# Moving three pieces of work around the gated recurrence of a hybrid backbone kernel: the third weight split, the order of the scans, and the gate rows

## The reference, cut to what matters

```python
xr, yr, qkv, z, beta_raw, alpha_raw = jnp.split(h @ w_in, EVEN_SPLITS, axis=-1)
xr = dw_conv(xr, lru_cw, lru_cb)
q, k, v = jnp.split(jax.nn.silu(dw_conv(qkv, dn_cw)), ...)

def lru_gates(xc, w_a, b_a, w_i, b_i, lam):       # for each of two directions d
    r = sigmoid(blockwise(xc, w_a) + b_a)
    i = sigmoid(blockwise(xc, w_i) + b_i)
    log_a = -LRU_C * r * softplus(-lam)
    a = exp(log_a)
    b = sqrt(-expm1(2.0 * log_a)) * (i * xc)
    return a, b                                   # then h[t] = a[t] * h[t-1] + b[t]
...
lru = (h_forward + h_backward) * gelu(yr)
```

## Time and profile before

| what | us |
|---|---|
| median of 3 runs | 1379.16 |
| lowest and highest of them | 1378.51, 1383.32 |
| the profiled execution's own time | 1377.73 |
| its span, first to last instruction | 1375.9 |
| PE busy | 1342.9 |
| DVE, ACT, POOL busy | 860.0, 693.1, 289.0 |
| recurrence's bodies b = 0 to 7 in the span | 84.7 to about 286 |

### The profile page before, as it was taken

How to read it: one execution, slowest core, us unless ns; L and a number is a source line. 1 busy time by engine, 2 the same in 40 slices (tenths; PEclk the granted TensorE clock), 3 DMA queues, 4 the chain that set the end, 5 groups by cost and what they waited for, 6 DMA issues and landing times.

```text
span 1375.9 us, 27903 instructions
## 1 busy us (share of the span) xinstructions
PE 1342.9 (98%) x11206; PEld 1265.3 (92%) x11206; DVE 860.0 (63%) x1320; ACT 693.1 (50%) x1100; POOL 289.0 (21%) x296
## 2 busy tenths in 40 slices
PE   6999999999999999999999999999999999999998
PEld 4889999998899999999899999999998988899997
DVE  4745889985456555543587666566736665664664
ACT  5367888868544455422533312343126665653543
POOL 2000124412566787621100000000120001100002
PEclk9999999999999999999999999999999999999999
DMA  9632232231411110123466566565423211455652
GB/s 326 200 86 85 78 92 77 78 93 62 143 43 32 59 35 31 63 77 100 138 194 192 183 197 190 184 197 180 138 92 122 93 62 47 154 183 185 187 188 99
DMA packets 138030, 170.88 MB, mean 124 GB/s; under 512 B 10912, under 2 KB 121760, under 8 KB 137920
## 3 DMA queue, kind: packets, MB, share of 16 engines
q1 hardware_dynamic: 137312, 169.13, 38.9%
q0 software_dynamic: 608, 0.19, 0.1%
HBM read 168.25 MB, written 1.05 MB: 123 GB/s over the span
## 4 chain that ended last, share of the span: by engine, by line
PE 81%; ACT 8%; DVE 5%; POOL 2%; issue 2%; DMA 1%; SPq 0%; ACTq 0%; POOLq 0%; DVEq 0%
PE bank L2324 59%; PE bank L2678 3%; PE bank L2666 3%; ACT w_hi L887 1%; PE bank L2250 1%; POOL qkv L741 1%; PE bank L2695 1%; DVE w_lo L1523 1%; DVE qkv L1565 1%; PE bank L2910 1%; ACT l_i L1153 1%; PE bank L2620 1%; PE bank L2933 1%; PE bank L2542 1%; PE bank L2644 1%
## 5 line engine op out<-in xcount | busy, mean ns | idle before, releaser
L1523 DVE TENSOR_TENSOR w_lo<-raw,w_hi 128x1024 fp32r<-128x1024 f32 x216 | 269.6, 1248 | 324.3 <-ACT w_hi L887 323.8
L887 ACT ACTIVATE w_hi<-raw 128x1024 fp32r<-128x1024 f32 x216 | 228.4, 1058 | 427.1 <-PE bank L2324 426.9
L2324 PE MATMUL bank<-h_hi,w_hi 128*128 128x256 f32 x1728 | 374.2, 283 | 13.6 <-DVE w_lo L1523 5.5
L2324 PE MATMUL bank<-h_hi,w_lo 128*128 128x256 f32 x1728 | 367.0, 279 | 0.0
L2324 PE MATMUL bank<-h_lo,w_hi 128*128 128x256 f32 x1728 | 359.9, 279 | 0.0
L2324 PEld LDWEIGHTS bank<-h_hi,w_hi 128*128 128x128 f32 x1728 | 277.2, 190 | 24.4 <-issue 16.7
L2324 PEld LDWEIGHTS bank<-h_hi,w_lo 128*128 128x128 f32 x1728 | 275.2, 189 | 0.0
L2324 PEld LDWEIGHTS bank<-h_lo,w_hi 128*128 128x128 f32 x1728 | 271.7, 189 | 0.3 <-DVE h_lo L1746 0.2
L709 POOL TENSOR_TENSOR n_sq<-xT 128x512 f32<-128x512 f32 (+1 forms) x24 | 23.3, 972 | 719.5 <-DVE xT L1593 718.6
L2324 PE MATMUL bank<-hid_hi,w_hi 128*128 128x256 f32 x768 | 172.9, 279 | 0.1
L2324 PE MATMUL bank<-hid_hi,w_lo 128*128 128x256 f32 x768 | 171.7, 278 | 0.0
(11 more groups left out here) (318 smaller groups left out, 2138.6 us busy)
## 6 DMA issues: line engine op xcount, KB each, us to landing
raw<-in_mlp_w SPq DMA_DIRECT2D x128, 512.0 KB, 3.6
late_w<-in_w_mod SPq DMA_DIRECT2D x56, 512.0 KB, 4.4
raw<-in_even_w_in SPq DMA_DIRECT2D x48, 512.0 KB, 3.7
raw<-in_w_mod SPq DMA_DIRECT2D x24, 512.0 KB, 4.4
first_w<-in_w_mod SPq DMA_DIRECT2D x16, 512.0 KB, 11.3
raw<-in_even_w_out SPq DMA_DIRECT2D x16, 512.0 KB, 3.4
raw<-in_attn_w_qkv SPq DMA_DIRECT2D x16, 512.0 KB, 3.6
raw<-in_attn_w_o SPq DMA_DIRECT2D x8, 512.0 KB, 3.5
```

What stands on the lines that cost most here:

```text
L887: act.activation(w_hi[:, j % SPLIT], raw[:, j % RAW], ACT.Copy).then_inc(hi_ready, 1)
L1523: dve.tensor_tensor(w_lo[:, j % SPLIT], raw[:, j % RAW], w_hi[:, j % SPLIT].bitcast(F32), ALU.subtract).then_inc(split_done, 1)
L2324: return pe.matmul(bank[2 * pair + t][:, c - n0:c - n0 + CTX], w[:, slot, k, t * P:(t + 1) * P], x_[:, c:c + CTX], start=(kk == 0 and firs ...
```

## The change

There are four edits.

1. PE: the gate rows and their signal `s_gps` move from behind `xr` to a place ahead of the fourth first unit (n = 3). The copy on ACT to `gate_f` moves with them, from behind `xr` to between its two bodies.
2. ACT: in bodies 0 to 7 the eight sigmoids are cut into two fours by direction, and the split of u2 goes between them.
3. ACT: the two tanhs go behind the split of u3, instead of ahead of it.
4. DVE: in all bodies but b = 8 the split of u2 goes ahead of `lru_output` of the tile before (its scans, sum and product), instead of behind it.

```diff
--- before.py
+++ after.py
@@ -1060,8 +1060,12 @@
                 ends = b == LRU_TILES + 1
                 beside(b, 0)
                 split_hi(u + 2, 2)
+                if b < LRU_TILES:
+                    lru_gates(b, 1)
                 beside(b, 1)
                 split_hi(u + 3, 3)
+                if b < LRU_TILES:
+                    lru_tanh(b)
                 evac(s, it, 0)
                 if b >= LRU_TILES:
                     value_silus(BY_POOL + 4 * (b - LRU_TILES))
@@ -1138,26 +1142,26 @@
 
                 act.wait_ge(s_lam, 1)
                 act.activation(sp_b[:, 64:80], sp_a[:, 64:80], ACT.Exp, scale=-1.0).then_inc(s_lam, 1)
+                act.wait_ge(s_gps, 1)
+                act.activation(gate_f[:, :], bank[X2][:, :], ACT.Copy).then_inc(s_gate, 1)
 
             segment(SEG["xr"], done=2, behind=decays_and_gates)
-            act.wait_ge(s_gps, 1)
-            act.activation(gate_f[:, :], bank[X2][:, :], ACT.Copy).then_inc(s_gate, 1)
-
-            def lru_gates(t_):
-
-                act.wait_ge(s_lps, t_ + 1)
-                act.wait_ge(l_w, t_)
-                act.wait_ge(l_x, t_)
+
+            def lru_gates(t_, d):
+
+                if d == 0:
+                    act.wait_ge(s_lps, t_ + 1)
+                    act.wait_ge(l_w, t_)
+                    act.wait_ge(l_x, t_)
 
                 def half_gate(out_, p0, q0, d, b, bias):
                     return act.activation(out_[q0:q0 + 64, d], bank[GATE_BANKS[2 * d + b]][p0:p0 + 64, :], ACT.Sigmoid, bias=bias[p0:p0 + 64, :])
 
-                for d in range(2):
-                    c_ = 8 * d + t_
-                    half_gate(l_y, 0, 0, d, 0, V("b_gate", c_))
-                    half_gate(l_i, 64, 0, d, 0, V("b_turn", c_)).then_inc(l_sig, 1)
-                    half_gate(l_i, 64, 64, d, 1, V("b_gate", c_))
-                    half_gate(l_y, 0, 64, d, 1, V("b_gate", 16 + c_)).then_inc(l_sig, 1)
+                c_ = 8 * d + t_
+                half_gate(l_y, 0, 0, d, 0, V("b_gate", c_))
+                half_gate(l_i, 64, 0, d, 0, V("b_turn", c_)).then_inc(l_sig, 1)
+                half_gate(l_i, 64, 64, d, 1, V("b_gate", c_))
+                half_gate(l_y, 0, 64, d, 1, V("b_gate", 16 + c_)).then_inc(l_sig, 1)
 
             def lru_decay(t_):
 
@@ -1166,6 +1170,9 @@
                 for d in range(2):
                     c_ = 8 * d + t_
                     act.activation(l_a[:, d], l_y[:, d], ACT.Exp, scale=lru_c[:, c_:c_ + 1]).then_inc(link_a, 1)
+
+            def lru_tanh(t_):
+
                 for d in range(2):
                     c_ = 8 * d + t_
                     acount[0] += 1
@@ -1196,7 +1203,7 @@
                     act.activation(gate_raw[:, :, :], gp, ACT.Copy).then_inc(s_gate, 1)
                 if b < LRU_TILES:
                     if w == 0:
-                        lru_gates(b)
+                        lru_gates(b, 0)
                     if w == 1:
                         lru_decay(b)
                     if w == 2:
@@ -1683,8 +1690,8 @@
                     split_lo(u + 2, 2)
                     beside(b, 0)
                 else:
+                    split_lo(u + 2, 2)
                     beside(b, 0)
-                    split_lo(u + 2, 2)
                 beside(b, 1)
                 split_lo(u + 3, 3)
                 evac(s, it, 0)
@@ -2473,7 +2480,17 @@
             half_flip(0)
             ready = normed("mix0")
             mods_beside = {(0, 0): 2, (0, 1): 1, (0, 2): 2, (1, 0): 2, (1, 1): 1}
+            def gate_rows():
+
+                pe.wait_ge(s_wg, 16)
+                for k in range(KT):
+                    r0 = 32 * (k % 4)
+                    mm = pe.matmul(bank[X2][r0:r0 + 32, :], wg[:, k], n_y[:, k], start=(k < 4), stop=(k >= 4), tile_position=(0, r0))
+                mm.then_inc(s_gps, 1)
+
             for n in range(4):
+                if n == 3:
+                    gate_rows()
                 pe.wait_ge(split_done, n + 1 + PRIME_SPLIT)
                 for k in range(UNIT_K):
                     first_rows_of(n, k, ready["ready"], ready["low"], 1 if (n, k) == (1, 2) else None)
@@ -2481,11 +2498,6 @@
             segment(SEG["xr"], h_hi, h_lo, 0, first=2 * SEG["xr"]["upp"], **ready)
             pe.wait_ge(s_ones, 16)
 
-            pe.wait_ge(s_wg, 16)
-            for k in range(KT):
-                r0 = 32 * (k % 4)
-                mm = pe.matmul(bank[X2][r0:r0 + 32, :], wg[:, k], n_y[:, k], start=(k < 4), stop=(k >= 4), tile_position=(0, r0))
-            mm.then_inc(s_gps, 1)
             def lru_gates(t_):
 
                 pe.wait_ge(evac_done, t_ + 1 + PRIME_EVAC)
```

## The result

| what | before | after |
|---|---|---|
| median of 7 runs each, us | 1379.16 | 1384.48 |
| lowest and highest | 1378.0, 1383.32 | 1382.68, 1385.21 |
| ratio, 95% interval | | 1.0028 [1.0018, 1.0039] |
| profiled execution's own time, span | 1377.73, 1375.9 | 1382.68, 1380.7 |

The change made the kernel slower, by 3.9 us by the ratio (2.5 to 5.4). The two medians of the table lie 5.3 apart, a quotient of 1.0039, at the upper end of that interval. The loss is inside half a per cent, but the median lies outside the range that was forecast (1376.5 to 1382.2).

What follows compares the result with a forecast made beforehand. PE was taken as the bound, busy 98% of the span. The 2.04 us lead and 1.69 stall won were to be absorbed, leaving +0.5: profiled 1377.73 to 1378.2, median 1379.16 to 1379.6 us, range 1376.5 to 1382.2.

Steps and rivals of the forecast that it cites:

- Edit 1: Moved gate rows fill PE's idle time; no wait for `gate_f`; first gate products at 82.64, 2.04 us earlier.
- the price per body: DVE's new order makes it later than ACT by 0.48 us per body, bodies 4 to 6.
- the sum of the ring: ACT and DVE's cycle from one body's exps to the next: 24.99 us before, 25.47 forecast for bodies 4 to 6.
- The other half: Part of the cycle from the exps to the split of the next u1, not worked out anew; only 10.08 became 10.56.
- edit 3 gives 0.5 back: Body 7, behind the exps: low split of u3 lies beside the tanhs, so the 1.3 us delay becomes 0.8.
- the lead: PE's gain from the gate rows, 2.0 us at first, shrinking from body 6 on and lost by the second sum.
- Body 7 and the second sum: Exps at 274.7; stall of 1.69 at u2 gone; PE waits for squares, second sum 298.22 becomes 298.8, +0.5 us.
- The new wait at u3 of body 7: Named sign of being right: new PE waits of 1 to 3 us for DVE at u1 or u3, bodies 6 and 7.
- Behind it ACT and DVE wait for PE again, so the shift stays: After the second sum of squares, the +0.5 us shift carries unchanged to the end.
- The bounds: PE's change no less than -4.64 us (every named stall gone); toward slower, +2.1 more.
- POOL's products reaching into the scans: Slower bound: cycle's price 1.0 instead of 0.48 per body, +2.1 us more; the slower rival had chance 0.12.
- The rule on the shared port: Read as leaving the low split unstretched beside POOL; rows said otherwise, 1.54 us used; unstretched rival 1378.3, chance 0.05.

Runs made afterwards that it cites:

- act_edits_masks: Edits 1 to 3 without DVE's reordering, plus POOL's four masked products held until the scans of tile 6 are done; 1375.28 us, 0.9966 of the kernel before.
- body9_alone: Kernel before, with DVE's split of u2 put ahead of the l2 norms' work in body 9 only; 1384.13 us, 1.0033 of before.
- act_edits: The changed kernel with all of DVE's order put back as before, so edits 1 to 3 only; 1375.4 us, 0.9973 of the kernel before.
- third_split_only: Edits 1 and 2 on the kernel before, with the tanhs still ahead of the split of u3 and DVE's order as before; 0.9991 of before.

## Why the prediction was wrong

**Edit 1: right.** No wait for `gate_f` and none ahead of the fourth first unit:

```profile
53.49 1.92 PE L2488 MATMUL bank<-n_y,wg 128*32 128x512 f32 x16
```

From the last product of the conditioning vector to the gates of body 2 the nine kernels with this edit take 89.71 to 90.26 us, the four profiles without it 91.63 to 92.47: their means differ by 2.15, forecast 2.04. (Between the two kernels of the forecast alone it is 1.78: the first gate products, forecast at 82.64, start at 83.43, in an execution whose conditioning vector ends 0.52 later.)

**Edit 4 in the recurrence: the price per body was right, the sum of the ring was not.** "Each body from 4 to 6 takes 24.99 + 0.48 = 25.47 us" failed. The half that was worked out (10.56) came as 10.62. The other half was taken as unchanged. The forecast had the very term that changes it ("edit 3 gives 0.5 back"), and used it in body 7 alone, although edit 3 stands in bodies 4 to 6 as well. It measured 0.56, and the two cancel. By the time of DVE's taps in body 2 the lead of 1.78 was down to 1.37, so the exps of body 3 came 0.24 earlier by the conditioning vector, where the forecast had 0.9.

**Body 7 and the second sum: right in the mechanism, in the times by luck.** The stall at u2 is gone, DVE's chain runs on into the squares, and the second sum waits for `sq`. POOL's part in it, argued from the rows, was shown by act_edits_masks. The times agree because errors cancel. Exps at 274.48 (forecast 274.7): DVE was through with the taps at 268.84 and not 269.7, its low split took 1.24 to the next start and not 1.54, and the scans, sum and product took 4.40 (270.08 to 274.48), where the forecast had 3.5. Second sum at 298.36 (forecast 298.8): by the conditioning vector it came 0.38 earlier than before, where the forecast had 0.58 later. An error of about 1 us, from the ring's sum and the lead above, is half hidden by an execution that began 0.52 later. The new wait at u3 of body 7 is 0.66, below the 1 to 3 us that were named.

**"Behind it ACT and DVE wait for PE again, so the shift stays": this is the step that failed.** It holds to the fifth sum (318.83 against 318.38, +0.45). At the sixth it is +3.49. The sentence on edit 4 ahead of the prediction said "in all bodies but b = 8", and the prediction costed it where scans stand beside the units. Body 9 was in the branch, and there the same two lines swap other work. In front of the split stood a pair of squares which needed nothing of it. Behind it they need ACT's high part, which comes at 325.37, since ACT makes roots and decays first. The rows for that were all in the trace of before: squares at 319.60, low split at 326.01, sum at 325.13. The squares that stood behind that split started at 327.48. Had those of the sixth sum stood there, the first would be done some 0.7 later, 3 us past the sum that needs it.

**The bounds.** Toward slower the forecast had only POOL's products reaching into the scans. It had no entry for a wait behind the second sum, so the range ended at 1382.2. With +3.0 at the sixth sum the working would have given 1378.2 + 3.0 = 1381.2 for the profiled execution, measured 1382.68, and 1379.6 + 3.0 = 1382.6 for the median, measured 1384.48. The 1.5 that is left in the profiled execution lies behind the first product of the delta net (+3.41 there, +4.8 at the end of the span). Half of it can be placed. PE's starts, matched one by one, are 3.50 us later than before at 660 us and 4.27 later at 700, and in between the changed kernel's profile has a stretch at the 1.2 GHz level which the profile of before lacks. Windows of before, then of the changed kernel:

```profile
680.00:684.00 4.00, 4.00 (x36) 4.00 (x35) 4.00 (x10) 2.56 (x6) 0.00 (x0) 1.00 0.20 82
684.00:688.00 4.00, 4.00 (x35) 3.86 (x33) 4.00 (x11) 3.00 (x7) 0.00 (x0) 1.00 0.00 0
```

```profile
680.00:684.00 4.00, 2.08 (x10) 2.11 (x11) 3.57 (x9) 2.86 (x7) 0.00 (x0) 0.77 0.72 240
684.00:688.00 4.00, 4.00 (x30) 4.00 (x30) 4.00 (x10) 2.55 (x7) 0.00 (x0) 0.80 0.06 23
```

The second profile of body9_alone, with no edit near that place, has such a stretch too (0.91 and 0.66 in the same windows), so it is no work of the change. What the medians have beyond 1382.6 stays open.

**The rule on the shared port.** The rows were right, and the prediction's reading of the rule was not. The low split takes 1.22 us alone and 2.06 beside POOL's products, `l_b<-l_b` 0.69 and 1.35, and POOL's product 1.05 and 2.02. The taps, one of whose two tensors comes from PSUM, take 4.01 us beside POOL's products and 4.02 without them. The prediction took from the Trainium skill (Advanced Engine Details and Errata, VectorE Performance Modes; VectorE: DVE Perf Modes, the perf-mode tier table) that an fp32 `tensor_tensor` is in no two-port mode, and concluded that GpSimd leaves it alone. The section GPSIMD Details of the same page, Advanced Engine Details and Errata, says more: GpSimd also conflicts with a DVE instruction that has two SBUF inputs. The split and the sum `l_b<-l_b` have two, and the trace agrees.

## What to carry to other kernels

An edit inside a branch acts wherever the branch is taken: list every pass of the loop that enters it, and cost the swap once for each kind of work that stands there. A wait moves ahead of all that was in front of it; in an order written by hand ask of each moved line what was ready without it. And when several engines form a ring, a saving found at one place of the period belongs into each period: work the whole ring out, both halves, before adding a price to it.

## What was not expected of the hardware

**PE has two paces at the same granted clock.** One body of the recurrence takes 24.79 us or 24.40, with the same instructions, no wait that the profile shows, and a granted clock of 1.00 in both. In act_edits:

```profile
234.06 1.99 PE L2513 MATMUL bank<-xc,lru_w 64*128 64x512 f32 x8
...
258.46 1.99 PE L2513 MATMUL bank<-xc,lru_w 64*128 64x512 f32 x8
```

and in the changed kernel:

```profile
233.41 1.99 PE L2513 MATMUL bank<-xc,lru_w 64*128 64x512 f32 x8
...
258.20 1.99 PE L2513 MATMUL bank<-xc,lru_w 64*128 64x512 f32 x8
```

Matmuls of line 2331 start 117.8 ns apart in the two units behind the gate products. From u2 on it is 113.3 ns in some bodies (act_edits above, from 247.7), 117.8 in others (all of the changed kernel's body). Over half a body, 96 matmuls, that is 0.43 us. The pace often changed at a short wait of PE at u2 (0.90 us in third_split_only), but not at all of them (0.24 in the next body of the same kernel), so the cause is open. It is as large as the terms that this forecast argued with.

**Half clock behind a stall.** In both profiles of body9_alone PE fell to the 1.2 GHz level right behind a wait of 2.9 us, for 1.7 and 1.8 us of lost time (granted clock 0.57 over 332 to 336 us in the first, over 328 to 332 in the second). Behind the same wait in the changed kernel it didn't (1.00 over 328 to 332). Stretches at that level stand elsewhere too, and not in every profile: at 680 to 688 us in that of the changed kernel and not in that of before. One such stretch costs as much as many of the steps that are argued here, so the granted clock belongs beside every comparison of two profiles.
